# AdaLN units 20 to 47 summed on VectorE and GpSimd inside the first MLP, TensorE only turning the sums

## The reference, cut to what matters

```
def ada_mods(cvec, w_ada, b_ada):
    m = jax.nn.silu(cvec) @ w_ada + b_ada
    return jnp.split(m[:, None, :], 6, axis=-1)
...
        sh1, sc1, g1, sh2, sc2, g2 = ada_mods(cvec, p['w_ada'][li], p['b_ada'][li])
        h = rms_norm(x, p['norm_w'][li, 0]) * (1 + sc1) + sh1
...
        h = rms_norm(x, p['norm_w'][li, 1]) * (1 + sc2) + sh2
        x = x + g2 * sq_relu_mlp(h, p['w_mlp1'][li], p['w_mlp2'][li])
```

## Time and profile before

| | |
|---|---|
| median of the runs | 1049.0 us |
| span of the profiled execution | 1047.8 us |
| TensorE busy | 1020.6 us, 97% |
| VectorE busy | 568.5 us, 54% |
| ScalarE busy | 486.1 us, 46% |
| GpSimd busy | 140.8 us, 13% |
| last residual of layer 0's mixers begins | 279.92 us |
| `split_low` of unit 19 (v = 2) begins, unit 19 follows | 296.38 us |
| first MLP ends | 562.85 us |

### The profile page before, as it was taken

One profiled execution on the slowest core, in us unless ns is written; L12 is line 12 of the kernel. 1 busy time (PEld: TensorE's weight loads), 2 busy tenths in 40 slices (PEclk: granted clock), 3 DMA queues, 4 the chain that ended last, 5 costly groups with the idle time before them and its releaser, 6 DMA issues.

```text
span 1047.8 us, 17863 instructions
## 1 busy us (share of the span) xinstructions
PE 1020.6 (97%) x7330; PEld 941.7 (90%) x7330; DVE 568.5 (54%) x914; ACT 486.1 (46%) x858; POOL 140.8 (13%) x173
## 2 busy tenths in 40 slices
PE   6999999999999999999999999999999999999997
PEld 3888885778999999999997989886999999999997
DVE  5556676564744345354457576576465445345452
ACT  5544665664553342342344556667464234252342
POOL 0162200011010010110110342350001011010110
PEclk9999999999999999999999999998999999999999
DMA  9987719645435445445445532223223524333311
GB/s 330 343 283 244 237 48 322 202 162 195 152 121 167 155 161 161 161 159 162 153 129 186 176 104 68 86 87 101 80 81 121 162 92 149 120 120 120 121 41 61
DMA packets 156974, 160.44 MB, mean 153 GB/s; under 512 B 3146, under 2 KB 155108, under 8 KB 156900
## 3 DMA queue, kind: packets, MB, share of 16 engines
q1 hardware_dynamic: 154512, 156.15, 45.0%
q0 software_dynamic: 704, 1.97, 0.6%
q10 hardware_dynamic: 1684, 1.26, 0.4%
HBM read 156.09 MB, written 3.28 MB: 152 GB/s over the span
## 4 chain that ended last, share of the span: by engine, by line
PE 92%; DVE 3%; ACT 2%; issue 1%; DMA 1%; SPq 0%; DVEq 0%; ACTq 0%
PE G L585 63%; PE G L590 13%; PE OB L607 4%; PE TB L554 4%; PE SC L918 2%; PE OB L932 1%; PE SC L694 1%; DMA raw<-in_w_ada 1%; PE OB L715 1%; PE OB L785 1%; PE TB L900 1%; ACT wH L1024 1%; PE SC L670 1%; PE SC L664 1%; PE SC L626 1%
## 5 line engine op out<-in xcount | busy, mean ns | idle before, releaser
L585 PE MATMUL G<-opH,wH 128*128 128x386 f32 (+1 forms) x768 | 267.7, 349 | 1.1 <-DVE wL L1505 0.8
L1024 ACT ACTIVATE wH<-raw 128x2048 fp32r<-128x2048 f32 x94 | 179.6, 1911 | 180.9 <-PE G L585 178.1
L585 PE MATMUL G<-opH,wL 128*128 128x386 f32 (+1 forms) x768 | 260.4, 339 | 0.0
L585 PE MATMUL G<-opL,wH 128*128 128x386 f32 (+1 forms) x768 | 260.2, 339 | 0.0
L1505 DVE TENSOR_TENSOR wL<-raw,wH 128x2048 fp32r<-128x2048 f32 x94 | 215.8, 2296 | 42.9 <-ACT wH L1024 42.9
L585 PE MATMUL G<-hidH,wH 128*128 128x384 f32 x512 | 173.3, 338 | 0.0
L585 PE MATMUL G<-hidH,wL 128*128 128x384 f32 x512 | 172.1, 336 | 0.0
L585 PE MATMUL G<-hidL,wH 128*128 128x384 f32 x512 | 172.1, 336 | 0.0
L585 PEld LDWEIGHTS G<-opH,wH 128*128 128x128 f32 x768 | 144.9, 189 | 9.8 <-issue 5.4
L585 PEld LDWEIGHTS G<-opL,wH 128*128 128x128 f32 x768 | 144.8, 189 | 1.6
L585 PEld LDWEIGHTS G<-opH,wL 128*128 128x128 f32 x768 | 144.9, 189 | 0.0
(11 more groups left out here) (246 smaller groups left out, 1192.6 us busy)
## 6 DMA issues: line engine op xcount, KB each, us to landing
raw<-in_w_mlp SPq DMA_DIRECT2D x64, 1024.0 KB, 5.2
raw<-in_w_ada SPq DMA_DIRECT2D x48, 1024.0 KB, 7.0
raw<-in_w_in_even SPq DMA_DIRECT2D x13, 1024.0 KB, 7.2
raw<-in_w_in_odd SPq DMA_DIRECT2D x12, 1024.0 KB, 5.1
raw<-in_w_out_even SPq DMA_DIRECT2D x4, 1024.0 KB, 6.6
raw<-in_w_out_odd SPq DMA_DIRECT2D x4, 1024.0 KB, 5.0
xin<-in_x_sample SPq DMA_DIRECT2D x2, 512.0 KB, 5.7
out_y_sample<-yout SPq DMA_DIRECT2D x1, 768.0 KB, 4.1
```

Of the source, the lines that this page charges most:

```text
L585: mm = pe.matmul(G[:, s, 512 * m:512 * m + cols], w[:, s, k, P * m:P * m + P], a[:, k, 0:cols], start=first and q == 0, stop=last and q == 2)
L1024: act.activation(wH[:, u % 2, :, :], raw[:, pos % RAW, :, :], ACT.Copy).then_inc(w_high, 1)
```

## The change

Units 20 to 47 leave the stream of `raw` buffers, the tables of jobs, and TensorE's `ada_mm`. They are 28 units, `LATE[n]` with n = 0 to 27, and each is loaded into one of four buffers `adaw` of its own. VectorE sums the eight row blocks of unit n, weighted with the first condition (`late_begin(n)`, eight instructions, each waiting for the one before); when that is done, GpSimd does the same for the second condition (`late_sum(n)`: eight products in place, then three additions of 1024, 512 and 256 columns). TensorE turns both sums (`late_turn(n)`, four transposes), and VectorE reduces the 512 columns that this gives and adds the bias (`late_mods(n)`). `late_begin` and `late_sum` of units 0 and 1 stand ahead of the first MLP; in round v follow `late_mods(v)` and `late_begin(v+2)` on VectorE, and `late_sum(v+2)` on GpSimd behind the square of round v.

```
+LATE = list(range(20, 48))
+SLOTS = 4
+EARLY_SUMS = 2
...
-    return [2 * u + 4, 2 * u + 5] + ([30 + u - 9] if u >= 9 else [])
+    return [2 * u + 4, 2 * u + 5] if u < 8 else []
...
-MLP_ADAS = {20: 36, 23: 37, 26: 38, 29: 39, 32: 40, 35: 41, 38: 42, 41: 43}
...
-ODD_ADAS = {2: [44, 45, 46, 47]}
...
+            def load_late(n):
+                if n == 0:
+                    sp.wait_ge(gemm_done, 14)
+                    sp.wait_ge(out_dma, 16 * 3)
+                if n >= SLOTS:
+                    sp.wait_ge(ada_summed, n - SLOTS + 1)
+                a = LATE[n]
+                sp.dma_start(adaw[:, n % SLOTS, :, :], unit_cols(t["w_ada"][a // ADA_COLS], (a % ADA_COLS) * UC)
+                             ).then_inc(adaw_in[n % SLOTS], 16)
...
+            def late_turn(n):
+                pe.wait_ge(ada_summed, n + 1)
+                take("tb", f"ada{LATE[n]}")
+                for c in range(2):
+                    for i in range(2):
+                        b = P * (2 * c + i)
+                        mm = turn(TB[:, b:b + P], adasum[:, n % SLOTS, c, P * i:P * i + P])
+                mm.then_inc(tb_full, 1)
...
-                        if base + i in MLP_ADAS:
-                            a = MLP_ADAS[base + i]
-                            middle = {1: lambda: ada_turn(a)} if half else {2: lambda: ada_mm(a)}
+                        v = base + i - U_MLP0
+                        if half and 0 <= v - 1 < len(LATE):
+                            middle = {**middle, 0: lambda n=v - 1: late_turn(n)}
...
+            def late_begin(n):
+                if n >= SLOTS:
+                    dve.wait_ge(tb_full, TB_USE[f"ada{LATE[n - SLOTS]}"] + 1)
+                dve.wait_ge(adaw_in[n % SLOTS], 16 * (n // SLOTS + 1))
+                acc = adasum[:, n % SLOTS, 0, :]
+                settle(dve.tensor_scalar(acc, adaw[:, n % SLOTS, 0, :], cst[:, 0, 0:1], None, ALU.mult))
+                for k in range(1, KT):
+                    ins = dve.scalar_tensor_tensor(acc, adaw[:, n % SLOTS, k, :], cst[:, k, 0:1], acc, ALU.mult, ALU.add)
+                    if k < KT - 1:
+                        settle(ins)
+                ins.then_inc(ada_begun, 1)
+            def late_mods(n):
+                a = LATE[n]
+                layer, j = a // ADA_COLS, 2 * (a % ADA_COLS)
+                full("tb", f"ada{a}")
+                dve.wait_ge(mods_set, a)
+                src = TB[:, :].rearrange("p (c i q) -> p i c q", c=2, i=2)
+                dve.tensor_reduce(adat, src, AX.X, ALU.add).then_inc(tb_free, 1)
...
             split_low(U_MLP0 + 1)
+            for n in range(EARLY_SUMS):
+                late_begin(n)
...
                     if i < ends:
                         split_low(u + 2, g)
-                    if u + 1 in MLP_ADAS:
-                        ada(MLP_ADAS[u + 1])
+                    if layer == 0:
+                        v = u - U_MLP0
+                        if v < len(LATE):
+                            late_mods(v)
+                        if v + EARLY_SUMS < len(LATE):
+                            late_begin(v + EARLY_SUMS)
...
+            def late_sum(n):
+                slot = n % SLOTS
+                pool.wait_ge(ada_begun, n + 1)
+                for k in range(KT):
+                    ins = pool.tensor_scalar(adaw[:, slot, k, :], adaw[:, slot, k, :], cst[:, k, 1:2], None, ALU.mult)
+                settle(ins)
+                for half in (4, 2):
+                    settle(pool.tensor_tensor(adaw[:, slot, 0:half, :], adaw[:, slot, 0:half, :],
+                                              adaw[:, slot, half:2 * half, :], ALU.add))
+                pool.tensor_tensor(adasum[:, slot, 1, :], adaw[:, slot, 0, :], adaw[:, slot, 1, :],
+                                   ALU.add).then_inc(ada_summed, 1)
+            for n in range(EARLY_SUMS):
+                late_sum(n)
+            for v in range(32):
+                i, q = v % 8, v // 8
+                if i < 4:
+                    u = U_MLP0 + v
+                    pool.wait_ge(relu_set, 4 * q + i + 1)
+                    if i >= 2:
+                        pool.wait_ge(hid_set, 4 * q + i - 1)
+                    pool.tensor_tensor(relu2[:, u % 2, :], relu[:, u % 2, :], relu[:, u % 2, :], ALU.mult).then_inc(relu2_set, 1)
+                if v + EARLY_SUMS < len(LATE):
+                    late_sum(v + EARLY_SUMS)
```

More of the change, by code:

```diff
@@ L231, in psum_uses @@
     sc.append("norm1")
-    for a in MLP_ADAS.values():
-        ob.append(f"ada{a}")
+    for a in LATE:
         tb.append(f"ada{a}")
@@ L328, in step_backbone_kernel @@
             ("mask32", [P, 5, 32], U8)])
-        hidH, hidL, relu, relu2, yout = arena([("hidH", [P, KT, NTOK], F32R), ("hidL", [P, KT, NTOK], F32R),
+        hidH, hidL, relu, relu2, yout, adaw, adasum = arena([("hidH", [P, KT, NTOK], F32R), ("hidL", [P, KT, NTOK], F32R),
                                          ("relu", [P, 2, 2 * NTOK], F32), ("relu2", [P, 2, 2 * NTOK], F32),
-                                         ("yout", [P, TT, D], F32)])
+                                         ("yout", [P, TT, D], F32),
+                                         ("adaw", [P, SLOTS, KT, UC], F32),
+                                         ("adasum", [P, SLOTS, 2, UC], F32)])
         (dqT, dkT, dv, dkc, dvc, draw, dsq, dout, DP, DW, DPT, doT, ropeO, lamp) = arena([
@@ L428, in step_backbone_kernel @@
         raw_in = [sem(f"raw_in{i}") for i in range(RAW)]
+        adaw_in = [sem(f"adaw_in{i}") for i in range(SLOTS)]
+        ada_begun, ada_summed = sem("ada_begun"), sem("ada_summed")
         w_high, w_split, gemm_done = (sem(n) for n in ("w_high", "w_split", "gemm_done"))
@@ L517, in _ @@
             for pos in range(POS["u", U_MLP0], POS["u", U_ODD]):
-                kind, n = STREAM[pos]
-                if kind == "a":
-                    load_ada(n)
-                else:
-                    load(mlp_unit(0, (n - U_MLP0) % 8, (n - U_MLP0) // 8), pos)
+                v = STREAM[pos][1] - U_MLP0
+                load(mlp_unit(0, v % 8, v // 8), pos)
+                if v == 2:
+                    for n in range(SLOTS):
+                        load_late(n)
+                if SLOTS <= v - 1 < len(LATE):
+                    load_late(v - 1)
             for pos in range(POS["u", U_ODD], POS["u", U_MLP1]):
-                kind, n = STREAM[pos]
-                if kind == "a":
-                    load_ada(n)
-                elif n < U_OUT_O:
+                n = STREAM[pos][1]
+                if n < U_OUT_O:
                     load(unit_cols(t["w_in_odd"][0], ODD_COLS[n - U_ODD]), pos)
@@ L2083, in relu_squares @@
                                        ALU.mult).then_inc(relu2_set, 1)
-            with pool.Fori(0, 4) as g:
-                relu_squares(U_MLP0, g, 0)
+            def late_sum(n):
[21 more added lines that the diff above has]
+                    late_sum(v + EARLY_SUMS)
             pool.wait_ge(rope_tab, 1)
```

99 lines of the change are left out of this document (48 added, 51 removed).

## The result

The changed kernel takes **1305.7 us** (median of 4 runs, 1303.6 to 1307.6), the kernel before 1049.0 in the same comparison: a ratio of **1.245**, 95% interval 1.243 to 1.247. The direction was predicted, the size was not: 1305.7 lies above the range of 1158 to 1270.

A forecast was written before the change was run, and what follows sets the result against it. TensorE, 97% busy, bounds the kernel before; queued sums (14 rounds at 17.3 us, 12 at 12.4) lengthen the first MLP by 175 us. 1047.8 + 175 - 14 = 1208.8, plus 1.2 to the median: 1210 us, range 1158 to 1270.

The forecast's parts named there:

- The sums end to end, the square behind them: First MLP's up rounds: `late_begin`, `late_sum`, then the square `relu2` needs, run in series; 17.3 us a round, 14 rounds.
- `late_sum`, 7.4 us: GpSimd's half per unit: eight products at 0.45 (3.6), additions 3.56, handing over 0.2; bounds 6.7 and 10.5 us.
- the upper bound of 0.84: Dearest price for one 256-column GpSimd product, taken from the row of 768 columns; 0.45 us was assumed.
- `late_sum` alone is over 9 us: Sign in the changed trace that would show the prediction wrong; `late_sum` was forecast at 7.4 us.
- its own upper bound of that term: `late_sum` at 10.5 us, with GpSimd's products at 0.84 each; the range left out most of this case.
- The estimate from the Trainium skill's figure in the prediction, 3.93: GpSimd's three additions at 2.2 ns a column, 3.93 us; total some 10 us longer; measured rows were preferred.
- products are dear: Rival: GpSimd's products at 0.84 each, `late_sum` 10.5 us, some 75 us more, 1285 us; chance 0.13.
- Exclusion: Down rounds: GpSimd's `late_sum` and VectorE's two-SBUF-input instructions keep each other out; 12.4 us a round instead of 8.9.
- twice 4 us: Expected sign: `late_begin` near 4 us when GpSimd stands, near twice that in a down round.
- down rounds under 10 us apart: Sign that would show the prediction wrong; down rounds of the first MLP were forecast 12 us apart.
- Savings outside: Gain outside the first MLP, 14 us: 12 in the mixers (of 0 to 19.5), 2 at layer 1's attention.
- The clock: Rival: TensorE's clock falls in its waits and stays down; down rounds 17.7 us, 64 us more, 1274 us; chance 0.07.

The follow-up runs named there:

- the run with two operations: Changed kernel with GpSimd's eight products as multiply and add 0.0 (two operations in one instruction) instead of multiply alone: 1220.4 us (one run).
- the version that won: Kernel before, with seven units (37 to 43) summed for both conditions by VectorE alone, one condition per down round: 1042.4 us, ratio 0.994.
- the broadcast product: Changed kernel with GpSimd's eight products as one tensor-by-tensor product of 2048 columns, the condition broadcast along the columns: 1233.9 us, ratio 1.176.
- the run with the order alone: Changed kernel with GpSimd's square of round v+1 queued ahead of the sum of unit v+2, all work kept: 1239.0 us, ratio 1.181.

## Why the prediction missed, step by step

**The sums end to end, the square behind them: right.** An up round by the changed kernel's rows: `late_sum` 336.85 to 348.65, 11.8; square 1.47; from the start of `hidL` to the end of `split_low` 3.15; `late_mods` 0.9; `late_begin` 4.0: 21.3, a tenth over the round's 21.2, because neighbours overlap by some hundredths. Every term but the first is close to what was predicted (1.47, 3.42, 0.9, 4.05).

**The step that failed is `late_sum`, 7.4 us:** "one line through both gives 0.50, and since the small one was a first call I take 0.45". The line went through an instruction with one operation (64 columns times a constant, 0.373) and one with two (768 columns, 0.84). The changed kernel's products have one. They took 0.906 (7.25 / 8), above even the upper bound of 0.84, which was the row of a form three times as cheap per column. The form was in the source line of each; I had put both under one name because the trace does. Products: 3.65 us over the 3.6 that I had. Of the prediction's signs of being wrong, "`late_sum` alone is over 9 us" came true with 11.8, and the range had left out its own upper bound of that term (10.5, which makes 1285). The additions too were dearer, by 0.8: 4.4 us against 3.56. The rows that I took for additions are products of every second element (line 2014), of 384 columns at most; the changed kernel's additions took 2.35, 1.27 and 0.72 us for 1024, 512 and 256 columns, 2.1 ns a column between the ends and not 1.67. The estimate from the Trainium skill's figure in the prediction, 3.93, was nearer than my line through two small ones, and still low.

In the form that the price belongs to, the prediction stands: the run with two operations (one run) gave up rounds of 17.7 us (17.3 predicted), down rounds of 11.9 (12.4), 1220.4 us (1210). That 0.45 is so near this form's 0.46 is luck, since the line had one end in each form. The rival "products are dear", 1285 us with a chance of 0.13, named the mechanism, at 0.84 and not 0.91.

**Exclusion: right in kind, wrong in who is held.** I let GpSimd's products hold VectorE for 0.2 us and VectorE hold GpSimd for about 0.3 six times, with VectorE done last. Products and multiply-adds of the changed kernel slow each other a little (in the down round above 8.17 us for eight products, 7.24 alone; 3.89 for seven multiply-adds, 3.61 alone), so `late_begin` did not come near twice 4 us. What keeps VectorE out is an addition: it and `split_low` stretch each other (5.66 for two, 3.68 alone; 4.41 for 2.29). With the dear products GpSimd is done last, and a down round is not VectorE's 12.4 us but GpSimd's: 8.2 for the products, 5.7 and 0.7 for the additions. Another sign of being wrong, down rounds under 10 us apart, came true for the first two of each group (8.2 us, then 8.7 to 9.1) and says little: VectorE ran ahead and paid at the next square. In the run with two operations the products are done sooner, and the multiply-adds meet the additions as forecast (2.52, 1.38 and 0.84 us in its chain, from 394.47 on), with VectorE last.

**Savings outside: too high.** `split_low` of unit 18 starts at 275.57 and not 284.76: the mixers gave 9.2 us, not 12. These are single executions; in the runs with the same mixers it starts between 273.75 and 279.86. From the end of the MLP on, 1301.8 - 817.8 = 484.0 us against 1047.8 - 562.85 = 484.95: 1 us, not 2.

**The clock: no part in it.** The granted clock was 0.78 on the mean from 290 to 735 us, but from 284 to 781 us no piece of the chain of waits is TensorE's; the page's line above shows the clock lower in the slices where TensorE waits for others.

The 93 us that were missing in the span (1301.8 - 1208.8): 14 up rounds at 3.9, 55; 12 down rounds at 2.0, 24; the start, 7 (two sums before round 0, by the same price); the end, 3; mixers and layer 1, 4.

## What to carry to other kernels

A price belongs to a form, not to an instruction's name: before a line is drawn through two rows, look at the source line of each for the number of operations, operands and where they lie. A second engine's idle time is not free work when what it has to do next is waited for: here GpSimd's part cost 224 us by its queue, its prices and the exclusion, and the version that won, with a quarter of the units, gave GpSimd nothing. Where two engines keep each other out, cheapening one's instruction or mending its order can hand the gain to the other's wait.

## What the runs showed of the hardware

- GpSimd's elementwise instruction with a scalar, float32: with one operation 0.91 us for 256 columns and 1.55 for 512 (0.82 for 256 with a constant), with two operations 0.46 for 256. Adding 0.0 is the cheaper instruction. The Trainium skill (GPSIMD Engine Reference, section Engine selection) calls GpSimd about half as fast as VectorE for two inputs and roughly at line rate for one; the runs don't agree for this form: VectorE's product of the same 256 columns took 0.35 us, so GpSimd took 2.6 times as long with one operation and 1.3 times with two.
- What keeps out VectorE's instructions with two inputs in SBUF is a GpSimd instruction with two inputs of its own (the additions, the broadcast product). Products with a scalar, of either form, do it hardly: a multiply-add of 0.50 took at most 0.59 beside one, and `hidL`, begun 0.05 us after a product in the run with the order alone, took its 0.96. They are held up themselves: beside a multiply-add 0.92 became up to 1.16 (one operation) and 0.46 became 0.64 (two), beside `split_low` 2.57 in both. One row of the kernel before is otherwise, the two-column addition of 0.74 us that ended with GpSimd's product of 768 columns. Why is open.
- Exclusion goes by whole instructions in the pairs seen here: `hidL` of 0.96 us took 4.35 beside a GpSimd product of 3.62 us; a multiply-add of 0.50 took 2.52 beside an addition. What to keep short is the other engine's single instruction.
